# Expert outputs of a decode step summed on chip by one-hot products, with sorted experts in triples

## The reference, cut to what matters

```python
def route_mix(t):                       # t: (320, 1024)
    p_grp = softmax(t @ w_grp); g_sel = argmax(p_grp); g_w = max(p_grp)
    le_g = (t @ w_exp) of the group g_sel                # 8 logits
    top_v, top_i = top_k(softmax(le_g), 2); top_v /= sum(top_v)
    combine = g_w * top_v at the two chosen experts, else 0      # (320, 32)
    hid = einsum('nd,edf->nef', t, w_ein)                # w_ein: (32, 1024, 512)
    a, b = split(hid, 2, axis=-1)
    act = silu(a) * b * combine[..., None]
    return einsum('nef,efd->nd', act, w_eout)            # w_eout: (32, 256, 1024)
x = x + g2 * hmoe(h2, ...)              # g2: per sequence and channel
y = rms_norm(x, norm_final_g)
```

## Time and profile before

| | us |
|---|---|
| median of three runs (lowest, highest) | 753.07 (752.62, 753.54) |
| the profiled execution: its own time | 755.45 |
| the profiled execution: span of its instructions | 753.8 |
| PE busy in the span | 696.9 (92%) |
| DVE, ACT, POOL busy | 278.3, 172.0, 84.5 |
| DMA moved | 236.15 MB, mean 313 GB/s |
| mean granted TensorE clock | 0.984 of full speed |

### The profile page before, as it was taken

The page is one execution under the profiler, slowest core; times in us unless marked ns, Lnnn a source line. Parts: engine busy times, 40 slices in busy tenths (PEclk is TensorE's granted clock), DMA queues, the critical chain, the costliest instruction groups (busy, mean ns, idle before and its releaser), DMA issues.

```text
span 753.8 us, 13479 instructions
## 1 busy us (share of the span) xinstructions
PE 696.9 (92%) x5136; PEld 398.8 (53%) x5136; DVE 278.3 (37%) x886; ACT 172.0 (23%) x410; POOL 84.5 (11%) x127
## 2 busy tenths in 40 slices
PE   5899899999999999799998999999999997888894
PEld 2687577558776665454555776664333332222342
DVE  2553123610102787664530322485411211111256
ACT  0223344112102564322242001331110101010102
POOL 0201000002500343110000000001212121112000
PEclk9999999999999999999999999999999999999998
DMA  8999997717344963899999992438999999999981
GB/s 239 383 411 396 410 366 236 309 68 276 113 157 180 359 256 120 313 363 389 392 378 385 420 407 87 191 104 312 419 418 418 418 419 417 419 419 418 420 254 72
DMA packets 63273, 236.15 MB, mean 313 GB/s; under 512 B 9733, under 2 KB 20878, under 8 KB 48293
## 3 DMA queue, kind: packets, MB, share of 16 engines
q1 hardware_dynamic: 52884, 218.73, 74.9%
q0 software_dynamic: 6432, 14.74, 5.3%
q10 hardware_dynamic: 3888, 1.77, 0.9%
HBM read 230.52 MB, written 19.14 MB: 331 GB/s over the span
## 4 chain that ended last, share of the span: by engine, by line
PE 62%; DMA 16%; SPq 13%; DVE 4%; issue 3%; ACTq 1%; ACT 1%; POOL 0%; POOLq 0%; DVEq 0%
PE bank L628 12%; SPq L485 7%; PE bank L1159 5%; PE bank L1038 5%; PE bank L1022 5%; SPq L504 4%; DMA arena<-in_w_eout 4%; DMA arena<-in_w_in 4%; PE bank L672 3%; PE bank L747 2%; PE bank L1186 2%; PE bank L565 2%; PE bank L970 2%; DMA arena<-h_rows,rows_of_slots_in 2%; PE bank L884 2%
## 5 line engine op out<-in xcount | busy, mean ns | idle before, releaser
L1159 PE MATMUL bank<-arena 128*32 128x512 f32 (+1 forms) x896 | 110.9, 610 | 14.2 <-DMA arena<-in_w_ein 14.0
L628 PE MATMUL bank<-arena 128*128 128x320 f32 x384 | 107.6, 439 | 2.8 <-DMA arena<-in_w_in 2.8
L628 PEld LDWEIGHTS bank<-arena 128*128 128x128 f32 x384 | 72.9, 191 | 34.7 <-DMA arena<-in_w_in 3.1
L1159 PEld LDWEIGHTS bank<-arena 128*32 128x32 f32 (+1 forms) x896 | 31.2, 114 | 82.9 <-issue 77.6
L1186 PE MATMUL bank<-arena 128*32 128x512 f32 (+1 forms) x464 | 58.3, 595 | 4.5 <-DMA arena<-in_w_eout 4.1
L2035 DVE COPY arena<-bank 128x512 f32<-128x512 f32 x14 | 9.7, 692 | 108.0 <-PE bank L1117 108.0
L1488 ACT ACTIVATE arena<-bank 128x256 f32<-128x256 f32 x16 | 6.2, 386 | 149.9 <-PE bank L1159 146.9
L1312 ACT ACTIVATE arena<-bank 32x320 f32<-32x320 f32 x60 | 25.8, 430 | 45.5 <-PE bank L628 45.0
L1038 PE MATMUL bank<-arena 128*128 128x320 f32 x128 | 35.0, 432 | 0.0
L1022 PE MATMUL bank<-arena 128*128 128x320 f32 x128 | 34.8, 432 | 0.0
L1186 PEld LDWEIGHTS bank<-arena 128*32 128x32 f32 (+1 forms) x464 | 15.6, 112 | 36.2 <-issue 29.8
(11 more groups left out here) (413 smaller groups left out, 1011.5 us busy)
## 6 DMA issues: line engine op xcount, KB each, us to landing
arena<-in_w_ein SPq DMA_DIRECT2D x52, 1024.0 KB, 25.2
arena<-in_w_eout SPq DMA_DIRECT2D x26, 1024.0 KB, 26.9
arena<-in_w_ada SPq DMA_DIRECT2D x12, 2048.0 KB, 14.3
arena<-in_w_in SPq DMA_DIRECT2D x10, 2048.0 KB, 10.4
arena<-in_k_pages SPq DMA_DIRECT2D x64, 320.0 KB, 6.0
arena<-in_v_pages SPq DMA_DIRECT2D x64, 320.0 KB, 9.2
arena<-in_w_ein SPq DMA_DIRECT2D x3, 4096.0 KB, 21.8
arena<-in_w_eout SPq DMA_DIRECT2D x3, 2048.0 KB, 13.1
```

The lines of the kernel that those rows point to most:

```text
L628: m = mm(banks[c % 4][:, 0:N], ring[q][:, k, P * (c % 4):P * (c % 4 + 1)], hT[:, k, :], start=(k == 0), stop=(k == KD - 1))
L1159: m = mm(banks[2 + p % 2][r:r + n, :], xeT[p % 2][:, k, r:r + n], wi2[p % 3][:, e, k, :], start=(k == 0), stop=(k == KD - 1))
```

## The change

The table `y_rows` goes, with its zeros, the scatters, the reading back and the sums of two rows. Every unit's output rows are added by products with one-hot tables, eight of 128 x 320 per unit (`by_token`), each followed by a `residual` on VectorE. Two PSUM banks (3 and 5) take these products in turn, so product c waits for the residual of product c-2. To free the banks, hidden products share bank 2 and turned activations share bank 4. `hits_of` makes the table of a unit on VectorE: 128 x 320, token number of the column equal to the token of the slot.

Sorted experts come in one pair (ranks 0 and 25, 96 and 32 slots) and eight triples (ranks p-3, p+5 and 28-p, with 64, 32 and 32 slots): 12 *units* instead of 16 pairs. The six weight places hold two triples: (2, 3, 4) and (5, 0, 1). Input weights of unit p (from 6 on) are loaded when the hidden layer of unit p-2 is done, output weights when its output layer is done. The output weights are stored so that a 512-column half lies together, and the last unit's come in two halves.

`CATCH_UP` says which units' rows are added inside which hidden layer: one unit's in 4, 5, 9, 10 and 11, two units' in 6, 7 and 8. Half of the products stand ahead of the hidden layer, the others one behind each chunk k. From unit 4 on TensorE's order is `hidden(p)`, `turn_rows(p+1)`, `turn_act(p)`, output of p. The rank arithmetic on VectorE has four operations more; the tables of slots have three less.

```diff
-        yR = at(M0, 3, 2, D)
-        last_hit, prev_hit = cst[:, C_COS:C_COS + N], cst[:, C_TRI:C_TRI + N]
+UNITS = 12
+CATCH_UP = {4: (0,), 5: (1,), 6: (2, 3), 7: (4, 5), 8: (6, 7), 9: (8,), 10: (9,), 11: (10,)}
+        hits = [cst[:, o:o + N] for o in (C_TRI, C_COS)]
+        LAST_BANKS = (0, 1, 3, 5, 2, 4, 6, 7)
+        def places_of(p):
+            if p < 4 or p >= UNITS:
+                return (0, 1) if p >= 3 else (2 * p, 2 * p + 1)
+            return (5, 0, 1) if p % 2 else (2, 3, 4)
@@ SyncE
-            for p in range(3, LAST - 1):
-                sorted_in(p + 1, after)
-                sorted_out(p, this)
-                this, after = after, sorted_pair(p + 2)
+            for p in range(6, UNITS):
+                of = experts_of(p)
+                sp.wait_ge(s_hd, p - 1)
+                unit_in(p, of, (0, 1, 2))
+                sp.wait_ge(s_od, 2 * (p - 1))
+                if p < LAST:
+                    unit_out(p, of, (0, 1, 2))
...
-            sp.wait_ge(s_ya, 1)
-            for half in range(2):
-                part = slice(512 * half, 512 * (half + 1))
-                for t, (t0, tn) in enumerate(TOK):
-                    for r in range(2):
-                        sp.dma_start(yR[0:tn, t, r, part], y_rows[N * r + t0:N * r + t0 + tn, part])\
-                            .then_inc(s_yl[3 * half + t], 16)
@@ TensorE
+            def by_token(p, c):
+                if c == 0:
+                    te.wait_ge(s_hm, p + 1)
+                    te.wait_ge(s_yA, p + 1)
+                if c == 4:
+                    te.wait_ge(s_yD, p + 1)
+                if 8 * p + c >= 2:
+                    te.wait_ge(s_x2, 8 * p + c - 1)
+                mm(banks[(3, 5)[c % 2]][:, 0:N], yeS[p % 4][:, P * c:P * (c + 1)], hits[p % 2], start=True, stop=True).then_inc(s_yt, 1)
-            def hidden(p, loaded=None):
+            def hidden(p):
+                pieces = [(q, c) for q in CATCH_UP.get(p, ()) for c in range(KD)]
+                ahead = len(pieces) // 2
+                for q, c in pieces[:ahead]:
+                    by_token(q, c)
...
                 for k in range(KD):
...
                     for r, n, e in tiles_of(p):
-                        m = mm(banks[2 + p % 2][r:r + n, :], xeT[p % 2][:, k, r:r + n], wi2[p % 3][:, e, k, :],
+                        m = mm(banks[3 if p == 1 else 2][r:r + n, :], xeT[p % 2][:, k, r:r + n], in_of(places_of(p)[e])[:, k, :],
                                start=(k == 0), stop=(k == KD - 1))
+                    if k == KD - 1:
+                        m.then_inc(s_hd, 1)
+                    elif len(pieces) > 8 or k < 4:
+                        for q, c in pieces[ahead + k:ahead + k + 1]:
+                            by_token(q, c)
+                for q, c in pieces[ahead + KD - 1:]:
+                    by_token(q, c)
...
-            for p in range(1, LAST):
+            for p in range(1, 4):
                 hidden(p)
...
-                pair_output(p - 1)
+                for half in range(2):
+                    unit_output(p - 1, half)
                 turn_act(p)
+            for half in range(2):
+                unit_output(3, half)
+            for p in range(4, LAST):
+                hidden(p)
+                turn_rows(p + 1)
+                turn_act(p)
+                for half in range(2):
+                    unit_output(p, half)
...
             with te.If(n_extra < 1):
-                tail()
+                unit_output(LAST, 0)
+                last_by_token(0)
+                unit_output(LAST, 1)
+                last_by_token(1)
+                square_sums()
@@ VectorE
+            def hits_of(p, n):
+                ve.tensor_scalar(hits[n], number, tokens[:, p:p + 1], None, ALU.is_equal).then_inc(s_hm, 1)
+            def by_token(p):
+                for c in range(KD):
+                    ve.wait_ge(s_yt, 8 * p + c + 1)
+                    residual(c, banks[(3, 5)[c % 2]], 40, s_x2, 8 * p)
...
+            for p in range(4, UNITS):
+                for q in CATCH_UP[p]:
+                    by_token(q)
+                if p < LAST:
+                    rows_out(p + 1)
+                for q in CATCH_UP.get(p + 1, (LAST,)):
+                    hits_of(q, q % 2)
+                pair_act(p)
+                act_out(p)
+                if p < LAST:
+                    pair_out(p)
@@ GpSimd
-            po.dma_start(y_rows.rearrange("(t p) d -> p t d", p=P),
-                         zeros.unsqueeze(1).to_broadcast([P, 2 * N // P, D])).then_inc(s_zf, 16)
...
-            for p in range(LAST - 1):
-                if p + 3 < PAIRS:
-                    gather(p + 3)
-                scatter(p)
+            for p in range(3, UNITS):
+                gather(p)
```

More of the change, by code:

```diff
@@ new lines, in _ @@
+            fourth = experts_of(4)
+            sp.wait_ge(s_hd, 1)
+            half_in(3, third, 1, (0, 1))
+            sp.wait_ge(s_hd, 2)
+            unit_in(4, fourth, (0, 1))
+            fifth = experts_of(5)
+            sp.wait_ge(s_od, 2)
+            unit_out(3, third, (0, 1))
+            sp.wait_ge(s_hd, 3)
+            unit_in(4, fourth, (2,))
+            unit_in(5, fifth, (0,))
+            sp.wait_ge(s_od, 4)
+            unit_out(4, fourth, (0, 1))
+            sp.wait_ge(s_hd, 4)
@@ L1106, in all_tables @@
                 for j in range(8):
[L1107 removed]
+                    m = mm(banks[6][:, 0:2 * ALLU], hit[0:RT, j, :], hitv[0:RT, j, :], start=(j == 0), stop=(j == 7))
                 m.then_inc(s_tab, 1)
@@ L1515, in _ @@
             rows_out(0)
-            for p in range(LAST):
+            for p in range(4):
                 if p:
@@ L1946, in _, with residual @@
             ve.wait_ge(s_x, 32)
-            def residual(c, bank, g0, s, before=0):
+            def residual(c, bank, g0, s, before=0, gated=None):
                 if before + c:
@@ L2222, in extra_pair @@
                 pair_out(p)
+                for c in range(KD):
+                    ve.wait_ge(s_yx, 8 * x + c + 1)
+                    residual(c, banks[5], 40, s_xr, 8 * x, s_xg)
+                ve.wait_ge(s_xr, 8 * (x + 1))
                 if x + 1 < EXTRA // 2:
@@ L2227, in tail @@
             def tail():
-                def row_sums(half, t):
-                    tn, part = TOK[t][1], slice(512 * half, 512 * (half + 1))
-                    ve.wait_ge(s_yl[3 * half + t], yl_before[3 * half + t] + 32)
-                    ve.tensor_tensor(yR[0:tn, t, 0, part], yR[0:tn, t, 0, part], yR[0:tn, t, 1, part], ALU.add).then_inc(s_ysum, 1)
-                def last_residual(first, last):
-                    for c in range(first, last):
-                        ve.wait_ge(s_yt, KD + c + 1)
-                        residual(c, banks[c], 40, s_x2, KD)
-                for t in range(3):
-                    row_sums(0, t)
-                row_sums(1, 0)
-                row_sums(1, 1)
-                last_residual(0, 1)
-                row_sums(1, 2)
-                last_residual(1, KD)
+                for c in range(KD):
+                    ve.wait_ge(s_yt, 8 * LAST + c + 1)
+                    residual(c, banks[LAST_BANKS[c]], 40, s_x2, 8 * LAST)
                 ve.wait_ge(s_ss3, 1)
```

392 lines of the change are left out of this document (195 added, 197 removed).

## The result

The changed kernel takes 780.02 us in the median of four runs (776.62 to 784.11), the kernel before 753.31 beside it: 1.035 times as long, 95% interval 1.031 to 1.039. The forecast was 761, range 750 to 771: the direction is right, the loss is more than three times as large. The profiled execution is the shortest of the four (776.62, span 774.9).

What follows compares the result with a forecast made beforehand. Weight loads of the sorted experts were taken to bound the kernel before. Output 3 at 554.8, plus 167.7 to output 10, then unit 11 and the tail to 765.2, less 4.0 for zeroing: 761.2 span, forecast 761, range 750 to 771.

Steps and rivals of the forecast that it cites:

- (a): Products ahead of the hidden layer, units 4 to 11: with two banks they run at VectorE's pace, a residual every 0.99 us.
- (b): Between tile groups of the hidden layer: each lone product costs 0.78 us instead of 0.54, for two changes of shape.
- (c): Units 4 to 11: pipelining is gone, so TensorE waits at hand-overs, 3.66 us from row turns to output in short units.
- the clock: Rival: TensorE falls to 1.2 GHz behind idle hand-overs; 765 to 766 for three units, 774 for all eight; chance 0.20.
- the units' sums: Output start to output start, units 4 to 10: 20.8 us with 8 products, 28.1 with 16; together 167.7.
- The tail: From the last unit's eighth residual to the end of the span: 11.9 us as before, nothing in there changes.
- The zeroing: Front, first long `w_in` wait: dropping the zeros of `y_rows` gains 4.0 us, bounds 0 and 4.5.
- Output of unit 3 starts ... 554.8: Start of unit 3's output layer: 555.4 from the earlier trace, less 0.6 for the tables, before the zeroing's gain.
- The loads: Rival: weight loads still set the end, 734 us of span, 733 on the median; chance 0.07.
- The shape changes: Rival: shape changes hide, a product between tile groups costs only 0.54 us; 751 of span, 750.7 median; chance 0.13.

Runs made afterwards that it cites:

- the pairs: Changed kernel with all products by token placed two together between the hidden layer's tile groups, none ahead: 766.12 us (1.014).
- the copies moved away: Changed kernel with only the two window-state copies on POOL's queue moved behind the wait for the rope, near 138 us: 780.57 us.
- the added wait: Changed kernel where SP issues the first half of unit 3's input weights only once unit 1's gather has landed: 772.78 us (1.025).
- gather and clock mended: Changed kernel with unit 3's input weights held until unit 1's gather landed, plus three unread products between row turns and activation turn in units 4 to 10: 765.64 us.
- without the products: Changed kernel without the products by token and residuals of units 0 to 10, all else kept: 743.95 us (0.985), span 741.7.
- the idle-time products: Changed kernel with three products that nothing reads between row turns and activation turn of units 4 to 10: 772.56 us (1.0225).
- the two fastest kernels: Changed kernel with old layer order, paired products, unread idle-time products, weights behind gather; the second ends the old order one unit earlier: 746.40 and 742.93 us.

## Why the prediction was right or wrong

*The three changes of order held.* (a) A residual starts every 0.98 us and sets the pace of the products ahead. (b) A lone product costs 0.74 instead of 0.54 between tile groups, 0.78 forecast, and a pair pays the difference once for two products (1.27 instead of 1.08). (c) The hand-over costs 3.50 (3.66 forecast), and putting the overlap back gives 2.2 us a unit. With the clock held up, output 3 to output 11 takes 189.3 us where the units' sums made 186.9: 2.4 too few, spread over eight units. The rule that the prediction takes from the Trainium skill, "TensorEngine Tiling (Array Packing)", section Key Properties, that a change of the tiling mode drains TensorE, agrees with the pairs: they change it once for two products.

*The tail was 1.2 short.* Everything up to the last residual came as forecast (eighth residual 11.6 us after output 11, both). Behind it "nothing changes" was wrong: 13.1 us instead of the 11.9 of the earlier trace rows. The square sums stand in TensorE's order behind the last four products and run in one block, 4.47 us to 764.7, so the next VectorE step comes 2.98 us after the eighth residual's start instead of 2.27. The other 0.5 stands behind the start of the last stores (5.87 us from there to the end, 5.41 before); why, no run shows.

*The zeroing was probably worth about 3, within its bounds, but not in the way forecast.* The term of 4.0 had the wait for the tile fall under 1 us and the products behind it run at full speed. In the changed kernel's profile the wait is 2.16 and the products are slow; of the twelve profiles without the zeroing and with early copies two have a wait under 1 us (0.38 and 0.86), and six have fast products. From 78 to 81 us the DMA engines move 1.20 MB, as many as before (1.21), now none of it on POOL's queue: other transfers filled the gap, which the forecast had as its lower bound. With the copies moved away the wait did go.

*The step that failed is "Output of unit 3 starts ... 554.8"*: it took the stretch from 490 to 555 us over from the trace before, as if nothing in it had changed but the tables. I costed SP's order from unit 4 on and passed over unit 3's first issue, which now meets the gather. From the products of three columns to output 3 the forecast has 54.1 us (554.8 less 500.69). The runs show 59.8 to 61.2 where the gather is met and 53.1 to 53.3 where neither it is met nor the half is slow, so the gather costs 6.5 us or more, and 7.2 in the medians. The changed kernel's profile doesn't show this wait, since there the slow hidden half took its place, 2.8 us; that its other runs met the gather is inferred from the profiles of the variants and from the gain of the added wait.

*The other term that failed is the clock, which the sum has at nothing.* It was a rival, with 0.20. From one wait of 1.43 us in the earlier trace rows that was not followed by a fall, I took it that hand-overs of 1.6 us would mostly be harmless. The hand-over has two idle times, though, 1.41 or 1.70 us and 0.56, with only the two products of the activation turn between them, and I had counted the first alone. Three to four of seven output layers fell in the changed kernel's order (units 6, 7 and 9 in its profile; 5, 6, 8 and 10 in that with the gather first), also behind a first wait of 1.41. The price was right: 1.70 each against 1.6. Its worth is 7 us: with either of the two terms mended alone the time is still 773.

In sum, for the profile with gather and clock mended: 761.2 forecast, + 2.4 units + 1.2 tail = 764.8, against a span of 765.0. That it closes so well is partly luck: output 3 stands at 550.82 there, where the forecast has 550.8, but the front varies by 4.7 us between profiles, and the stretch behind it was 1 us shorter than forecast. On medians the same sum is 764.1 against 765.6; + 7 gather + 7 clock on the measured 765.6 gives 779.6, against 780.0.

*The loads* did not set the end of the changed kernel, as forecast; where they did, without the products, it came at 742, 8 above what I worked out for that rival. *The shape changes* did not hide.

## What to carry to other kernels

Where overlap between layers is given up, price the idle hand-over twice: once as time, once as what TensorE's clock does behind it, and take a single harmless wait in the trace for no proof. Work in that gap that nobody reads is a cheap test, and was worth 7 us here. When a diff reorders a queue, follow every issue of it to the moment it now falls on, also where the code around it looks the same: three register reads moved behind one issue cost 4 us by the medians and 6.5 in the profiles, nearly the whole loss that was forecast. And a gain in bytes at one place can be taken back at the next: copies moved away from one tile were followed by a wait for another.

## What was not expected of the hardware

TensorE's clock fell with hardly an idle time before. In the changed kernel's profile the granted clock is 0.57 from 500 to 508 us, though TensorE counts as busy for all 8.00 us:

```profile
500.00:508.00 8.00, 8.00 (x29) 3.55 (x28) 7.29 (x29) 0.07 (x1) 1.15 (x1) 0.57 0.08 12
```

Its last idle time before was 0.36 us, at 495.60:

```profile
495.60 3.84 PE L1114 MATMUL bank<-arena 80*128 80x128 f32 x32 [0.36 <-DVE arena L2169]
```

What it did right before the fall were sixteen products of three columns; the hidden half behind them ran in 6.47 us instead of 3.65, mostly at 1.2 GHz. The same products stand in the kernel before and in that of the idle-time products, and no fall follows (3.65). Of the changed kernel and its fourteen variants five profiles show it, the two fastest kernels' among them. Why some executions fall there and others not stays open.
